# Strassen's seven products for queries, keys and merge gates in a hybrid decoder block

## The chip, the cores and the metric

The kernel runs on one core of a Trainium2 chip. The metric is the device time of one execution in microseconds (us), the median over repeated executions; lower is better.

## The reference, cut to what matters

One decoder layer over 1,024 tokens of width 1,024, in float32. The part that the change touches is the input projection `z = u @ w_in`, whose columns belong to seven consumers:

```python
u = rms_norm(x, g_mix)
z = u @ w_in
xr, gr, q, k, v, fl, m_lru, m_attn = split(z)      # 1024 columns each, fl has 8
h = rg_lru(causal_depthwise_conv(xr, ...), ...)     # gates from xc, then a linear recurrence in time
y_lru = (h * gelu(gr)) @ w_lru_out
log_f = log_sigmoid(fl + b_forget)                  # its running sum is a bias of the attention scores
o = forgetting_attention(q, k, v, log_f)            # 8 heads of 128
merged = sigmoid(m_lru) * y_lru + sigmoid(m_attn) * (o @ w_attn_out)
x = x + merged @ w_out
x = x + hierarchical_moe(rms_norm(x, g_ffn), ...)   # 32 experts, two for each token
out = rms_norm(x, g_final)
```

## The kernel before

Every float32 matrix product is made of three products of a 32-bit format that TensorE takes quickly: each operand is split into a high and a low part, and high by high, high by low and low by high are summed. ScalarE makes a high part by a copy, VectorE the low part by a subtraction. `u` is held turned, as `uh` and `ul` (128 partitions, 8 chunks of the width, 1,024 tokens).

The projection is made in blocks of 256 columns of `w_in`. `load_block` brings a block into one of two slots, `split_hi` and `split_lo` split it. `product` makes 128 of its columns against all tokens: 8 chunks x 3 products x 2 token halves = 48 matmuls of 128x512. A block is two such products, `c` = 0 and 1. `product_rows` (values) has tokens on the partitions: 24 matmuls of 128x256 for each of 8 token tiles of a block.

The stages follow each other with a barrier of all engines at the end of each (`stage`):

- `norm_in` (line 215): RMSNorm, turning and splitting of `u`, and the first product of the next stage.
- `lru_qk` (line 356): four turns. Each makes a block of XR, a block of GR, the 48 matmuls of the recurrence's gates (line 465), a block of keys and a block of queries. The convolution, the gates' functions and the recurrence's scan (lines 557 to 586) run on VectorE and ScalarE beside the products of the same turn.
- `value` (line 596): four blocks of values, 32 tiles.
- `merge_gates` (line 672): eight blocks of merge gates with a sigmoid, and the forget gate: 48 matmuls with 8 columns of `w_in` as weights, its logarithm on 8 partitions x 1,024 tokens, its running sum by a scan.
- `branch_out(0)` (line 813): splits `mix`, the recurrence's output, into `uh` and `ul`, and multiplies by `w_lru_out`. Then follow `attention`, `branch_out(1)`, `project_route` and `experts`, untouched but for two waits.

Stages are tied over their barriers in this way: the last product that TensorE makes in a stage is often the first of the next one, so that TensorE has work up to the barrier. `merge_gates` has none after its last block, and `branch_out(0)` can't start before it has split `mix`. Queries, keys, values and gates go to DRAM (`qk_d`, `v_d`, `sig_d`) and are read back in later stages. The semaphores of these stores outlive a stage.

Of the kernel before, what the change touches and what calls it, by code (L numbers as in the profile page):

```python
# [26 lines left out]
F32 = mybir.dt.float32  # L27
# [23 lines left out]
NEG = -3.0e38  # L51

# [38 lines left out]
class Kernel:  # L91
    def __init__(self, nc, ins, out):
# [47 lines left out]
        self.v_mm = [self.sem(f"v_mm{s}") for s in range(2)]  # L140
# [7 lines left out]
        self.sig_stored = [stores(f"sig{s}") for s in range(2)]  # L148
# [66 lines left out]
    def norm_in(self):  # L215
# [23 lines left out]
        with nc.Block() as block:  # L239
            @block.sync  # L240
            def _(sp):
                for t in range(NT):
                    sp.dma_start(xt[:, t, :], k_.x[t * P:(t + 1) * P, :]).then_inc(x_loaded[t], 16)
                for s, col in enumerate((XR, GR)):
                    k_.load_block(sp, s, 0, k_.w_block(k_.w_in, col))
# [110 lines left out]
    def lru_qk(self):  # L356
# [5 lines left out]
        p0, self.pairs = self.pairs, self.pairs + 2 * turns  # L362
# [16 lines left out]
        st = [work.put(f"qk_{c}", [P, 2, T], F32R) for c in range(2)]  # L379
        SCALE = (1.0, -HD ** -0.5)  # L380
# [4 lines left out]

        qk_hi, qk_lo = ([[sem(f"qk_{n}{g}{c}") for c in range(2)] for g in range(2)] for n in ("hi", "lo"))
        qk_stored = k_.qk_stored
# [7 lines left out]
        w_c = (k_.w_first, k_.w_used)  # L395

        with nc.Block() as block:
            @block.sync
            def _(sp):
                def gates(i):  # L400
                    sp.wait_ge(rg_lo, i)
# [3 lines left out]
                def store(i, g, c):  # L405
                    sp.wait_ge(qk_lo[g][c], i + 1)
                    part = 2 - 2 * g

                    head = 2 * i + c if g == 0 else i + i + c
                    sp.dma_start(k_.qk_d[head][:, part:part + 2, :], st[c][:, :, :].bitcast(F32))\  # L410
                        .then_inc(qk_stored[c], 16)

                def turn(i, last):
                    for s, col in enumerate((KC, QC)):
                        k_.load_block(sp, s, p0 + 2 * i + 1, k_.w_block(k_.w_in, col + WB * i))
                    if not last:
                        gates(i + 1)
                    for s, col in enumerate((XR, GR)):
                        store(i, s, 0)
                        k_.load_block(sp, s, p0 + 2 * i + 2, k_.w_block(k_.w_in, VC + WB * s if last else col + WB + WB * i))  # L420
                        store(i, s, 1)
                gates(0)
                with sp.Fori(0, turns - 1) as i:
                    turn(i, False)
                turn(turns - 1, True)

            @block.gpsimd
            def _(pool):
# [5 lines left out]
                for i in range(turns):  # L434
                    for ready in (*xr_out, *gr_out, *qk_hi[0]):
                        if blocks == MAXX:
                            break
                        pool.wait_ge(ready, i + 1)
# [7 lines left out]
            def _(pe):  # L446
                def products(i, s, pair, read, count, cs=(0, 1)):

                    pe.wait_ge(k_.w_lo[s], p0 + 2 * i + pair + 1)
                    for c in cs:  # L450
                        pe.wait_ge(read[c], count)
                        k_.product(pe, k_.ps[c], s, c).then_inc(w_c[c][s], 1)

                def turn(i):
                    products(i, 1, 0, xr_out, i + 1)
                    pe.wait_ge(rg_lo, i + 1)
                    pe.wait_ge(xcl_done, 2 * i + 2)
                    for m in range(2):
                        for g in range(2):
                            pe.wait_ge(gate_out[g], 2 * i + m)  # L460
                            for kk in range(2):
                                for w, u, first, last in ((rg_h, xc_h, kk == 0, False), (rg_h, xc_l, False, False),
                                                          (rg_l, xc_h, False, kk == 1)):
                                    for h in range(2):
                                        mm = pe.matmul(k_.ps[2 + g][:, h * HALF:(h + 1) * HALF],
# [3 lines left out]
                    products(i, 0, 1, gr_out, i + 1)  # L469
                    products(i, 1, 1, qk_lo[0], i + 1)  # L470

                products(0, 0, 0, qk_lo[1], 0, (1,))
                turn(0)
                with pe.Fori(1, turns) as i:
                    products(i, 0, 0, qk_lo[1], i)
                    turn(i)
                pe.wait_ge(k_.w_lo[0], self.pairs + 1)
                for g in range(2):
                    pe.wait_ge(gate_out[g], 2 * turns)
                for t in range(2):  # L480
                    k_.product_rows(pe, k_.value_ps(t), 0, t, k_.uh, k_.ul).then_inc((k_.w_first[0], k_.v_mm[0])[t], 1)

            @block.scalar
            def _(act):
                def xr_copy(i, c):
                    act.wait_ge(w_c[c][0], p0 + 2 * i + 1)
                    act.activation(xr[:, c, pad:pad + T], k_.ps[c][:, :], ACT.Copy).then_inc(xr_out[c], 1)
# [5 lines left out]
                def gelu(i, c):  # L493
                    act.wait_ge(w_c[c][1], p0 + 2 * i + 1)
                    act.activation(gl[:, c, :], k_.ps[c][:, :], ACT.Gelu_apprx_tanh).then_inc(gr_out[c], 1)

                def qk_high(i, g, c):
                    act.wait_ge(w_c[c][g], p0 + 2 * i + 2)
                    act.wait_ge(qk_stored[c], 16 * (2 * i + g))
                    act.activation(st[c][:, 0, :], k_.ps[c][:, :], ACT.Copy, scale=SCALE[g]).then_inc(qk_hi[g][c], 1)  # L500

                with act.Fori(0, turns) as i:
                    k_.split_hi(act, 1, p0 + 2 * i)
                    act.wait_ge(mixed, 2 * i)
                    xr_copy(i, 0)
                    act.wait_ge(rg_loaded, 32 * (i + 1))
                    act.wait_ge(gate_mm[1], 2 * i)
# [3 lines left out]
                    k_.split_hi(act, 0, p0 + 2 * i + 1)  # L511
# [3 lines left out]
                    for m in range(2):  # L515
                        act.wait_ge(gate_mm[0], 2 * i + m + 1)
                        act.activation(a_sb[:, m, :], k_.ps[2][:, :], ACT.Sigmoid, bias=cur[:, m, PBA:PBA + 1])\
                            .then_inc(gate_out[0], 1)
                        act.wait_ge(gate_mm[1], 2 * i + m + 1)
                        act.activation(i_sb[:, m, :], k_.ps[3][:, :], ACT.Sigmoid, bias=cur[:, m, PBX:PBX + 1])\  # L520
                            .then_inc(gate_out[1], 1)
                    for m in range(2):
                        act.wait_ge(gate_out[0], 2 * i + m + 1)
                        act.activation(rt_sb[:, m, :], a_sb[:, m, :], ACT.Tanh, scale=cur[:, m, PS:PS + 1])\
                            .then_inc(t_done, 1)
                    for m in range(2):
                        act.wait_ge(t_done, 2 * i + m + 1)
                        act.activation(a_sb[:, m, :], a_sb[:, m, :], ACT.Exp, scale=cur[:, m, PN:PN + 1])\
                            .then_inc(a_done, 1)
                    act.activation(rt_sb[:, :, :], rt_sb[:, :, :], ACT.Sqrt).then_inc(root, 1)  # L530
                    k_.split_hi(act, 1, p0 + 2 * i + 1)
                    for c in range(2):
                        qk_high(i, 0, c)
                    k_.split_hi(act, 0, p0 + 2 * i + 2)
                    for c in range(2):
                        qk_high(i, 1, c)

            @block.vector
            def _(dve):
                PER = 15  # L540

                def qk_low(i, g, c):
                    dve.wait_ge(qk_hi[g][c], i + 1)
                    dve.scalar_tensor_tensor(out=st[c][:, 1, :], in0=k_.ps[c][:, :], scalar=SCALE[g],
                                             in1=st[c][:, 0, :].bitcast(F32), op0=ALU.mult,
                                             op1=ALU.subtract).then_inc(qk_lo[g][c], 1)

                dve.wait_ge(zeroed, 1)
                with dve.Fori(0, turns) as i:
                    steps = Steps(dve, own, i * PER)  # L550
                    dve.wait_ge(a_done, 2 * i)
# [1578 lines left out]
```

## Time and profile before

| what | value |
|---|---|
| median of 3 runs | 1825.11 us (1822.89 to 1829.03) |
| profiled execution: its time, its span | 1828.22 us, 1826.5 us |
| busy share of the span | TensorE matmul 93%, VectorE 57%, ScalarE 46% |
| mean granted TensorE clock | 0.973 of full speed |
| `lru_qk`, `value`, `merge_gates` | 42.5 to 707.5 us, TensorE busy 660.6 of 665.0 us |
| experts | from 1204.7 us on, DMA busy 98% |

TensorE's matmuls are pipelined: one of 128x512 lasts 390 ns in the profile, but the next one starts before it ends. The price of one is therefore the distance of starts, read from rows of the timeline. A granted clock of 1.00 is 2.4 GHz and one of 0.5 is 1.2 GHz.

### The profile page before, as it was taken

What the parts mean: (1) busy time and instruction counts of PE and PEld (TensorE: products, weight loads), DVE (VectorE), ACT (ScalarE), POOL (GpSimd) and SP (SyncE); (2) the same over time, 40 slices, a digit from 0 to 9 for tenths busy, and PEclk for the clock granted to TensorE, in tenths of its full rate; (3) what the DMA queues carried; (4) which work ended last, traced back from release to release, by engine and by line L of the source; (5) the groups of instructions that cost most, each with busy time, mean ns of one, the idle gap of its engine ahead of it and who ended that gap; (6) DMA issues with size and microseconds to landing.
All of it is one profiled execution on the core that took longest, in us unless ns stands there. A gap on an engine that the chain in (4) does not pass through costs nothing. (4 is left out here: it accounts for less than half of the span.)

```text
span 1826.5 us, 22589 instructions
## 1 busy us (share of the span) xinstructions
PE 1703.8 (93%) x8515; PEld 1364.1 (75%) x8515; DVE 1037.0 (57%) x1125; ACT 840.3 (46%) x845; POOL 137.6 (8%) x187
## 2 busy tenths in 40 slices
PE   5999999999999998999888999969999999999991
PEld 4888888889987887878777888846667777777760
DVE  4353444432213313247665433769988888888886
ACT  5433334241122212036553111247777777878772
POOL 1000000000000000011110000110000000000005
PEclk9999999999999999999999999979999999999995
DMA  4343333323331223546655240379999999999977
GB/s 151 93 153 95 109 96 131 115 100 111 134 132 63 92 93 137 183 154 230 212 170 180 92 166 36 121 285 391 399 390 398 392 398 392 392 399 392 398 293 280
DMA packets 151686, 390.36 MB, mean 214 GB/s; under 512 B 14009, under 2 KB 73481, under 8 KB 147537
## 3 DMA queue, kind: packets, MB, share of 16 engines
q1 hardware_dynamic: 138368, 343.20, 51.0%
q0 software_dynamic: 8384, 29.63, 5.1%
q10 hardware_dynamic: 4880, 16.82, 2.3%
q8 instruction: 34, 0.56, 0.1%
q14 instruction: 20, 0.16, 0.0%
HBM read 322.15 MB, written 67.46 MB: 213 GB/s over the span
## 5 line engine op out<-in xcount | busy, mean ns | idle before, releaser
L1608 DVE TENSOR_TENSOR e_l<-e_raw,e_h 128x2048 fp32r<-128x2048 f32 x192 | 439.2, 2290 | 64.8 <-ACT e_h L1602 64.5
L1602 ACT ACTIVATE e_h<-e_raw 128x2048 fp32r<-128x2048 f32 x192 | 367.8, 1917 | 84.9 <-PE ps L1637 50.2
L199 PE MATMUL ps<-uh,w_h 128*128 128x512 f32 x1008 | 312.9, 392 | 11.9 <-DVE ul L908 9.7
L199 PE MATMUL ps<-ul,w_h 128*128 128x512 f32 x1008 | 312.1, 391 | 0.0
L199 PE MATMUL ps<-uh,w_l 128*128 128x512 f32 x1008 | 311.7, 391 | 0.0
L183 DVE TENSOR_TENSOR w_l<-w_raw,w_h 128x2048 fp32r<-128x2048 f32 x38 | 87.1, 2292 | 328.5 <-ACT w_h L179 328.5
L199 PEld LDWEIGHTS ps<-uh,w_h 128*128 128x128 f32 x1008 | 189.8, 189 | 52.8 <-issue 13.2
L199 PEld LDWEIGHTS ps<-ul,w_h 128*128 128x128 f32 x1008 | 190.2, 189 | 39.8
L199 PEld LDWEIGHTS ps<-uh,w_l 128*128 128x128 f32 x1008 | 190.2, 189 | 39.7
L1624 PE MATMUL ps<-e_h,e_xth 128*96 128x512 f32 x512 | 205.1, 401 | 6.3 <-DVE e_l L1608 3.0
L1624 PE MATMUL ps<-e_h,e_xtl 128*96 128x512 f32 x512 | 202.6, 396 | 0.0
L1624 PE MATMUL ps<-e_l,e_xth 128*96 128x512 f32 x512 | 201.9, 394 | 0.0
L179 ACT ACTIVATE w_h<-w_raw 128x2048 fp32r<-128x2048 f32 x38 | 72.7, 1914 | 167.6 <-DMA w_raw<-w_in 82.6
L1624 PEld LDWEIGHTS ps<-e_h,e_xth 128*96 128x96 f32 x512 | 83.0, 162 | 46.4 <-issue 7.3
L1624 PEld LDWEIGHTS ps<-e_h,e_xtl 128*96 128x96 f32 x512 | 83.1, 162 | 36.0
L1624 PEld LDWEIGHTS ps<-e_l,e_xth 128*96 128x96 f32 x512 | 83.4, 163 | 31.9
L1637 PE MATMUL ps<-e_h,e_hth 128*96 128x512 f32 x256 | 82.6, 404 | 2.1 <-DVE e_htl L1758 2.1
L1637 PE MATMUL ps<-e_l,e_hth 128*96 128x512 f32 x256 | 80.3, 395 | 0.0
L1637 PE MATMUL ps<-e_h,e_htl 128*96 128x512 f32 x256 | 80.2, 394 | 0.0
L1689 POOL DMA_INDIRECT e_xg<-xn_d,slots_i x30 | 41.3, 1378 | 474.2 <-PE ps L1700 474.2
L211 PE MATMUL ps<-w_h,uh 128*128 128x256 f32 x256 | 72.6, 284 | 0.9 <-PEq L164 0.9
L1097 PE MATMUL ps<-at_qk 128*128 128x512 f32 (+3 forms) x288 | 71.2, 378 | 2.3 <-PEq L164 2.0
(285 smaller groups left out, 2375.3 us busy)
## 6 DMA issues: line engine op xcount, KB each, us to landing
e_raw<-w_exp_gate SPq DMA_DIRECT2D x64, 1024.0 KB, 20.2
e_raw<-w_exp_up SPq DMA_DIRECT2D x64, 1024.0 KB, 20.1
e_raw<-w_exp_down SPq DMA_DIRECT2D x64, 1024.0 KB, 19.5
w_raw<-w_in SPq DMA_DIRECT2D x28, 1024.0 KB, 5.6
qk_d<-qk SPq DMA_DIRECT2D x16, 1024.0 KB, 4.2
at_qk<-qk_d SPq DMA_DIRECT2D x8, 2048.0 KB, 11.6
y_d<-e_y ACTq DMA_DIRECT2D x32, 384.0 KB, 6.5
y_d<-zeros POOLq DMA_DIRECT2D x22, 384.0 KB, 4.2
```

The lines of the kernel that those rows point to most:

```text
L179: act.activation(self.w_h[s][:, :, :], self.w_raw[s][:, :, :], ACT.Copy).then_inc(self.w_hi[s], 1)
L183: dve.tensor_tensor(self.w_l[s][:, :, :], self.w_raw[s][:, :, :], self.w_h[s][:, :, :].bitcast(F32), ALU.subtract).then_inc(self.w_lo[s], 1)
L199: mm = pe.matmul(ps[:, h * HALF:(h + 1) * HALF], w[:, k, :], u[:, k, h * HALF:(h + 1) * HALF], start=first, stop=last)
L211: mm = pe.matmul(ps, u[:, k, rows], w[s][:, k, :], start=first, stop=last)
L1097: mm = pe.matmul(k_.ps[n % 2][:, at:end], q, qk[c][:, part, at:end], start=first, stop=last)
L1602: act.activation(self.e_h[m % SPLIT][:, :, :], self.e_raw[slot][:, :, :], ACT.Copy).then_inc(self.e_hi[m % SPLIT], 1)
L1608: dve.tensor_tensor(self.e_l[slot][:, :, :], self.e_raw[slot][:, :, :], self.e_h[m % SPLIT][:, :, :].bitcast(F32), ALU.subtract).then_inc( ...
L1624: mm = pe.matmul(ps, x[:, k, :], w[:, k, :], start=first and first_piece, stop=last and last_piece)
L1637: mm = pe.matmul(ps[:, c * HALF:(c + 1) * HALF], x[:, at, :], w[:, 2 * k + c, :], start=first, stop=last)
L1689: pool.indirect_dma_start(out=xg[b][:, :], out_offset=None, in_=k_.xn_d, in_offset=bass.IndirectOffsetOnAxis(ap=slots, axis=0)).then_inc(g ...
```

## The change

Four stages take the place of `lru_qk`, `value` and `merge_gates`; three barriers stay three.

- `first_heads`: keys and queries of the first head pair by `product` as before, the forget gate's 48 matmuls between them, its logarithm and sum now with tokens on 128 partitions (64 elements each) and the sum by two small matmuls; and VectorE makes the four sums T1 to T4 of the quarters of `u` (width halves x token halves) and splits them.
- `halves`: the other three head pairs of keys and queries and all merge gates, 14 blocks, each as Strassen-Winograd's seven half products of 12 matmuls (4 chunks x 3) instead of two products of 48. For each block VectorE makes 4 sums of the quarters of the block, 7 low parts, 7 additions of products into the four quadrants of the result, and for keys and queries 4 low parts of the result; ScalarE 7 high parts, a copy and 4 finishing copies or sigmoids. All are 128x512. Operands go round a ring of 11 tiles, products round 6 PSUM banks, the raw block has one place.
- `lru_value`: four turns of XR, GR, the recurrence's gates and one block of values. The recurrence's scan runs beside the values. Loops are written out instead of `Fori`.
- `branch_out(0)` waits for the new stores' semaphores.

```diff
+HALVED = [(kind, i) for i in range(1, D // WB) for kind in "KQ"] + [(kind, i) for i in range(D // WB) for kind in "LA"]
+RING = 11
+USED = ("A11", "S1", "S2", "A12", "S3", "S4", "A22")
+MADE = ("A11", "S1", "S2", "A12", "A22", "S3", "S4")
+BANKS = 6
+    def load_quarters(self, eng, n):
+        for c in range(2):
+            eng.dma_start(self.raw_q[:, 2 * c:2 * c + 2, :, :].rearrange("p q k n -> p (q k) n"),
+                          self.w_in.rearrange("(k p) n -> p k n", p=P)[:, :, col + c * P:col + (c + 1) * P])\
+                .then_inc(self.raw_in, 16)
+    def first_heads(self):      # SyncE
+                store(0, 0)
+                sp.wait_ge(k_.w_used[0], p0 + 1)
+                k_.load_quarters(sp, 0)
+                store(0, 1)
+                for c in range(2):
+                    store(1, c)
+                sp.wait_ge(bias_out, 1)
+                sp.dma_start(k_.bias_d.rearrange("h (t p) -> (h t) p", p=P), bias[:, :]).then_inc(k_.bias_stored, 16)
+                for c in range(2):
+                    sp.wait_ge(qk_stored[c], 16 * 2)
...
+                # VectorE, the end of first_heads
+                turned_low(T4, 4)
+                low(1, 0)
+                dve.wait_ge(f_turned, 1)
...
+                dve.wait_ge(sum_mm, 1)
+                dve.tensor_tensor(flat(c_sum), sum_ps, flat(fr), ALU.add).then_inc(sum_out, 1)
+                low(1, 1)
+    def halves(self):           # SyncE
+                def load(n):
+                    sp.wait_ge(a_lo, 7 * n - 7 + MADE.index("A22") + 1)
+                    if n < NBLOCKS:
+                        k_.load_quarters(sp, n)
+                    else:
+                        k_.load_block(sp, 0, p0, k_.w_block(k_.w_in, XR))
+                load(1)
+                for n in range(NBLOCKS):
+                    store(n, C11)
+                    if n + 2 <= NBLOCKS:
+                        load(n + 2)
+                    for q in (C22, C12, C21):
+                        store(n, q)
...
+                # TensorE
+                def part_product(n, name):
+                    pe.wait_ge(a_lo, 7 * n + MADE.index(name) + 1)
+                    bank_free(n, name)
+                    for k in range(KD // 2):
+                        for w, u, first, last in ((r_h, u_h, k == 0, False), (r_h, u_l, False, False),
+                                                  (r_l, u_h, False, k == KD // 2 - 1)):
+                            op = pe.matmul(bank(n, name), w(n, name)[:, k, :], u[:, k, :], start=first, stop=last)
+                    op.then_inc(mm, 1)
...
+                # ScalarE
+                for n in range(NBLOCKS):
+                    copy(n)
+                    high(n + 1, "A11")
+                    for name in ("S1", "S2", "A12"):
+                        high(n + 1, name)
+                    finish(n, C11)
+                    high(n + 1, "A22")
+                    finish(n, C22)
+                    high(n + 1, "S3")
+                    finish(n, C12)
+                    high(n + 1, "S4")
+                    finish(n, C21)
...
+                # VectorE
+                for n in range(NBLOCKS):
+                    for name in SUMS:
+                        add_up(n + 1, name)
+                    low(n + 1, "A11")
+                    join(n, 1, C12, C11, "S2")
+                    low(n + 1, "S1")
+                    join(n, 2, C11, C11, "A12")
+                    low(n + 1, "S2")
+                    low(n + 1, "A12")
+                    final_low(n, C11)
+                    join(n, 3, C21, C12, "S3")
+                    join(n, 4, C12, C12, "S1")
+                    join(n, 5, C22, C21, "S1")
+                    low(n + 1, "A22")
+                    low(n + 1, "S3")
+                    final_low(n, C22)
+                    join(n, 6, C12, C12, "S4")
+                    low(n + 1, "S4")
+                    final_low(n, C12)
+                    join(n, 7, C21, C21, "A22")
+                    final_low(n, C21)
+    def lru_value(self):        # TensorE
+                for i in range(turns):
+                    products(i, OF_XR, gr_out, i, (0, 1) if i > 0 else (1,))
+                    products(i, OF_GR, xr_out, i + 1)
+                    gates(i)
+                    values(i)
...
                     for m in range(2):
                         steps.did(dve.scalar_tensor_tensor(out=rt, in0=a, scalar=1.0, in1=rt, op0=ALU.add, op1=ALU.mult))
                         steps.did(dve.tensor_tensor(i_sb[:, m, :], i_sb[:, m, :], rt, ALU.mult))
+                        value_low(i, 3 + 2 * m)
+                        if m == 0:
+                            k_.split_lo(dve, *slot(i, NEXT))
                         steps.did(dve.tensor_tensor_scan(rt, a, i_sb[:, m, :], 0.0, ALU.mult, ALU.add))
+                        value_low(i, 4 + 2 * m)
+                        dve.tensor_tensor(k_.mix[:, 2 * i + m, :], rt, gl[:, m, :], ALU.mult).then_inc(mixed, 1)
+                    value_low(i, NT - 1)
...
+                for c in range(2):      # SyncE, the end of lru_value
+                    sp.wait_ge(k_.v_stored[c], 16 * NH // 2)
```

## Rows read from the trace of the kernel before

**Rows 1.** The page, busy time of TensorE's matmuls: us, share, count.
```profile
PE 1703.8 (93%) x8515; PEld 1364.1 (75%) x8515; DVE 1037.0 (57%) x1125; ACT 840.3 (46%) x845; POOL 137.6 (8%) x187
```

**Rows 2.** Busy time by stretch: lru_qk, value, merge_gates; clock, DMA share, GB/s last.
```profile
42.50:425.00 382.50, 382.47 (x1680) 315.72 (x1681) 162.42 (x119) 141.45 (x115) 17.75 (x23) 1.00 0.33 111
425.00:530.60 105.60, 103.53 (x818) 101.09 (x817) 23.16 (x37) 20.05 (x37) 0.00 (x0) 1.00 0.40 140
530.60:707.50 176.90, 174.55 (x768) 139.36 (x768) 38.48 (x22) 41.30 (x33) 0.95 (x1) 1.00 0.27 85
```

**Rows 3.** Timeline of TensorE (start, us): matmuls in norm_in and in the recurrence's gates.
```profile
35.95 0.39 PE L310 MATMUL ps<-uh,w_h 128*128 128x512 f32 x1
...
40.71 0.39 PE L310 MATMUL ps<-uh,w_h 128*128 128x512 f32 x1
...
75.29 0.63 PE L465 MATMUL ps<-lru_xch,rg_h 128*128 128x512 f32 x2
...
86.06 0.64 PE L465 MATMUL ps<-lru_xch,rg_l 128*128 128x512 f32 x2
```

**Rows 4.** Timeline of ScalarE: high parts of two neighbouring value tiles.
```profile
515.65 0.38 ACT L651 ACTIVATE v<-ps 128x256 fp32r<-128x256 f32 x1 [2.50 <-PE ps L211]
518.53 0.38 ACT L651 ACTIVATE v<-ps 128x256 fp32r<-128x256 f32 x1 [2.50 <-PE ps L211]
```

**Rows 5.** Timeline of ScalarE in the first turn of lru_qk.
```profile
86.73 1.12 ACT L520 ACTIVATE lru_xr<-ps,lru_prm 128x1024 f32<-128x1024 f32 x1 [1.70 <-PE ps L465]
87.75 2.18 ACT L524 ACTIVATE lru_rt<-lru_a,lru_prm 128x1024 f32<-128x1024 f32 x2
89.94 1.28 ACT L528 ACT_TABLE_LOAD   x1
91.24 2.19 ACT L528 ACTIVATE lru_a<-lru_a,lru_prm 128x1024 f32<-128x1024 f32 x2
...
94.74 1.92 ACT L530 ACTIVATE lru_rt<-lru_rt 128x2048 f32<-128x2048 f32 x1
```

**Rows 6.** Timeline at the barrier before branch_out(0).
```profile
704.55 0.61 PE L199 MATMUL ps<-uh,w_l 128*128 128x512 f32 x2
705.21 1.02 ACT L763 ACTIVATE m<-ps 128x1024 f32<-128x1024 f32 x1 [9.85 <-PE ps L199]
707.55 7.69 ACT L890 ACTIVATE uh<-mix 128x1024 fp32r<-128x1024 f32 x8 [1.32 <-PEq L164]
710.01 1.19 PE L199 MATMUL ps<-uh,w_h 128*128 128x512 f32 x2 [4.84 <-DVE ul L908]
...
713.45 0.62 PE L199 MATMUL ps<-ul,w_h 128*128 128x512 f32 x2
```

**Rows 7.** Groups of instructions by line and shape: busy us, mean ns, idle before.
```profile
L1161 DVE TENSOR_TENSOR at_ptl<-ps,at_pth 128x512 fp32r<-128x512 f32 x48 | 32.3, 688 | 1.4 <-ACT at_pth L1140 1.2
L328 DVE SCALAR_TENSOR_TENSOR ul<-ps,gm,uh 128x512 fp32r<-128x512 f32 x16 | 11.0, 745 | 0.2
L1140 ACT ACTIVATE at_pth<-ps 128x512 fp32r<-128x512 f32 x48 | 27.8, 596 | 12.5 <-PE ps L1106 12.5
L782 DVE TENSOR_TENSOR f_l<-f_raw,f_h 128x64 fp32r<-128x64 f32 x1 | 0.2, 218 | 0.0
L584 DVE TENSOR_TENSOR lru_xr<-lru_xr,lru_rt 128x1024 f32<-128x1024 f32 x8 | 9.8, 1225 | 0.3
L585 DVE TENSOR_TENSOR_SCAN lru_rt<-lru_a,lru_xr 128x1024 f32<-128x1024 f32 x8 | 18.3, 2292 | 0.3
```

**Rows 8.** DMA issues of a stretch: count, KB each, median us from issue to landing.
```profile
qk_d<-qk SPq DMA_DIRECT2D x16, 1024.0 KB, 4.2
v_d<-v SPq DMA_DIRECT2D x8, 1024.0 KB, 9.2
at_v<-v_d SPq DMA_DIRECT2D x2, 512.0 KB, 6.3
at_v<-v_d SPq DMA_DIRECT2D x2, 512.0 KB, 15.4
```

More of the change, by code:

```diff
@@ L354, in _, with halves_map @@
                 dve.tensor_scalar(k_.prm[:, :, PN], eq[:, :], -LRU_C, None, ALU.mult).then_inc(own, 1)
-    def lru_qk(self):
+    def halves_map(self):
+        turned = Map(self.nc, self.work_start - 4 * KD * T, self.high)
+        self.t_h, self.t_l = ([turned.put(f"wn_t{n}{part}", [P, KD // 2, HALF], F32R) for n in range(1, 5)] for part in "hl")
+        self.halves_at = turned.at
+        same = Map(self.nc, self.work_start - 4 * KD * T, self.high)
+        self.t_spare, self.t_full = ([same.put(f"wn_t{n}{part}", [P, KD // 2, HALF]) for n in range(1, 5)] for part in ("spare", "full"))
@@ L378, in lru_qk @@
         gl = work.put("lru_gl", [P, 2, T])
-        st = [work.put(f"qk_{c}", [P, 2, T], F32R) for c in range(2)]
-        SCALE = (1.0, -HD ** -0.5)
+        vst = [work.put(f"v_{part}", [P, NT, WB], F32R) for part in range(2)]
         sem = self.sem
@@ L413, in turn, with load @@
-                def turn(i, last):
-                    for s, col in enumerate((KC, QC)):
-                        k_.load_block(sp, s, p0 + 2 * i + 1, k_.w_block(k_.w_in, col + WB * i))
+                def load(i, kind, src):
+                    s, p = slot(i, kind)
+                    k_.load_block(sp, s, p, src)
+                gates(0)
+                for q in range(4):
+                    sp.wait_ge(k_.quad_stored[q], 16 * k_.quads_until(NBLOCKS))
+                load(0, OF_GR, k_.w_block(k_.w_in, GR))
@@ L416, in turn @@
+                for i in range(turns):
+                    load(i, OF_V, k_.w_block(k_.w_in, VC + WB * i))
+                    last = i == turns - 1
+                    load(i, NEXT, k_.w_block(k_.ins["w_lru_out"][0], 0) if last else k_.w_block(k_.w_in, XR + WB * (i + 1)))
                     if not last:
                         gates(i + 1)
[L418 to L425, printed above, removed]
+                    load(i + 1, OF_GR, k_.w_block(k_.ins["w_lru_out"][0], WB) if last else k_.w_block(k_.w_in, GR + WB * (i + 1)))
+                    for t in range(4):
+                        sp.wait_ge(v_lo[t], 2 * i + 2)
+                    for part in range(2):
+                        sp.dma_start(k_.v_d[i, part], vst[part][:, :, :].bitcast(F32)).then_inc(k_.v_stored[i % 2], 16)
@@ L446, in _, with products, gates @@
             def _(pe):
-                def products(i, s, pair, read, count, cs=(0, 1)):
-                    pe.wait_ge(k_.w_lo[s], p0 + 2 * i + pair + 1)
+                def products(i, kind, read, count, cs=(0, 1)):
+                    s, p = slot(i, kind)
+                    pe.wait_ge(k_.w_lo[s], p + 1)
                     for c in cs:
[L451 to L455, printed above, removed]
+                        if count > 0:
+                            pe.wait_ge(read[c], count)
+                        k_.product(pe, in_ps[c], s, c).then_inc(w_c[c][s], 1)
+                def gates(i):
                     pe.wait_ge(rg_lo, i + 1)
@@ L2105, in write @@
     def write(self):
-        for write, *args in ((self.norm_in,), (self.lru_qk,), (self.value,), (self.merge_gates,),
+        for write, *args in ((self.norm_in,), (self.first_heads,), (self.halves,), (self.lru_value,),
                              (self.branch_out, 0), (self.attention,), (self.branch_out, 1), (self.project_route,),
```

646 lines of the change are left out of this document (372 added, 274 removed).

## The prediction, made before the change was run

> **What bounds the kernel now.** I read the page first: TensorE's matmuls fill 93% of the span [rows 1]. A share over the whole span says little, so the second view is busy time by stretch. In the three stages that change, TensorE is idle for 0.03 us of 382.5, 2.07 of 105.6 and 2.35 of 176.9, all at full clock, while VectorE and ScalarE are busy for 20 to 40% of it [rows 2]. These 665 us are therefore a queue of matmuls: one that is left out is worth its full distance of starts, and every new pause of TensorE costs its full length. The third view gives that distance. The reader is to see that starts, not durations, count: 21 matmuls lie between 35.95 and 40.71 us, 0.2267 us each, and this is the form that the change uses, one 512-column matmul for each weight [rows 3]. The recurrence's gates are slower, 46 between 75.29 and 86.06, 0.2341 us [rows 3]. A value tile takes 2.88 us [rows 4].
>
> **What is taken away.** A block takes 84 matmuls instead of 96. 14 blocks save 168 x 0.2267 = **38.1 us**. XR, GR, values, the first head pair, the forget gate (48 matmuls) and the recurrence's gates keep their counts. A block of `halves` lasts 84 x 0.2267 = 19.04 us, a half product 2.72 us, and 14 blocks 266.6 us.
>
> **Does `halves` keep TensorE fed?** VectorE has 22 operations of 128x512 in a key or query block and 18 in a gate block. The nearest row is 0.69 us [rows 7] (L1161); with a wait on its own predecessor some 0.03 more. 22 x 0.69 = 15.2 us. Three times it must stand still for ScalarE, whose 128x512 takes 0.60 us [rows 7] (L1140): the low part of S3 comes after `finish(C22)` and its own high part (two operations, 1.2, one of VectorE's beside them, so 0.5), that of S4 after `finish(C12)` (1.2), the last `final_low` after `finish(C21)` (0.6). That makes 17.6 us against 19.04. The chain that could stop TensorE is a bank: A11 of the next block needs the bank of S1, read last by join 5. S3's product ends at 13.6 us of the block, three joins later it is 15.8, and the bank is wanted at 19.04: 3.2 us to spare. Operands are ready more than 9 us ahead. At the 0.745 of L328 [rows 7] the cycle is 16.4 + 2.3 + waits = 19.0, still level. I take nothing, and keep up to +7 us for the range.
>
> The raw block has one place. Its load is issued after the low part of A22 and wanted by the sum S1: 15 VectorE operations (10.4 us) and the landing must fit into 19.04, so the landing may take 8.5 us. The nearest row is the pair of loads with 512-byte pieces, 2 x 512 KB: 6.3 us, and 15.4 in the worst case beside other transfers [rows 8]. I take 6.3 (the quiet queue is the likelier likeness: stores of 1.5 MB follow it, they do not precede it), so nothing; the upper end is a rival below. ScalarE has 12 x 0.60 = 7.2 us in a block.
>
> The start costs something. The first load is issued only when the first block's A22 is split; VectorE waits for it and reaches join 5 about 0.5 us late; S1's low part is 0.5 late; and after a pause the clock is at its lower level: from 710.01 to 713.45 eight matmuls took 3.44 us instead of 1.81 [rows 6], 1.6 more. **+2.6 us.**
>
> **The end of `first_heads`.** Count from its start. TensorE: K's second product, forget gate, Q's first, 3 x 10.88 = 32.7; eight small transposes 0.7; Q's second: 44.3 us. VectorE starts at 3.2 (one copy, one split on ScalarE); eight sums and five splits of 2,048 elements (twice a 1,024-element L584 less its start, 2.3 [rows 7]) are 30.3; two low parts and the bias addition 3.8; the next low part 1.2: 38.5. Then the forget gate's chain: some 12 operations of 64 elements at 0.22 [rows 7] (L782), a reciprocal, seven smaller ones, and on ScalarE two table loads of 1.28 [rows 5] with a short activation each: 7 us, 45.5. Two small matmuls, one addition, the last low part: 47.2. The store that follows takes 4.2 [rows 8], and SyncE waits for it before the barrier; the barrier itself 1.3 (from 706.23 to 707.55 [rows 6]); the first high and low part of `halves` 1.4: 54.1. TensorE stands for 9.8 us, less 0.1 for its small matmuls, and 0.7 earlier: 10.4. The old barrier there cost 0.9 of the 2.07 us: **+9.5 us**. In short, a chain on VectorE and a store that were hidden behind eight more blocks are now the last thing before a barrier. Bounds: 7 (the sums overlap the start better) and 13.
>
> Of table loads, the Trainium skill (ScalarE: Activation LUTs, What ACT_TABLE_LOAD costs) says that each switch drains the engine for about 1.38 us beside the load. The trace shows no such time: the tanh ends at 89.93, the load starts at 89.94 and the exponential at 91.24 [rows 5]. By the page the sum would be 2.8 us higher; by the row it is as above.
>
> **`halves` to `lru_value`.** XR's first product is made before the barrier and hides the last stores. Behind it GR's load waits for those stores and for two small loads in SyncE's queue; with 6.3 landing, a split of 1.9 and 2.3, GR is ready at about the time when TensorE ends XR (10.9 us). Barrier 1.1 and 0.5 of waiting against 1.2 for the old one: **+0.4 us**. Bounds 0 and +4.
>
> **A turn of `lru_value`.** Gates 11.25 us, eight tiles 23.0. Tile 7 needs the low part of tile 3. Count from the gates' start, 75.29 in the old turn: the last sigmoid starts at 11.4, as before [rows 5]. ScalarE now waits for tile 2 (20.1) ahead of the root, which ends at 23.7 instead of 21.4. VectorE then has two recurrence steps, the low part of tile 3 (26.6) and so on; TensorE wants tile 7's bank at 31.4. No wait, nothing.
>
> **The end of `lru_value`.** From 23.7 VectorE has, for two halves, 2 x 1.23, a scan 2.3, a product 1.2 [rows 7] (L584, L585), five low parts of 0.42 and one block split 2.3: 40.2. TensorE's last tile ended at 34.3. Then SyncE stores 2 x 1 MB and waits. One such store alone takes 4.2, two behind another megabyte 9.2 [rows 8]; halfway, 6.7, and 0.5 for the second issue: 47.5. Barrier 1.3; first split of `mix`, 2.46 until TensorE starts (707.55 to 710.01 [rows 6]): 51.3. TensorE stands 17.0 us where it stood 5.0 (704.94 to 710.01): **+12.0 us**. Bounds +8 and +15. The recurrence's tail and the values' store had four and two further stages to hide in; now `branch_out(0)`, which needs `mix` and starts with an empty TensorE, follows directly.
>
> **Sum.** -38.1 + 2.6 + 9.5 + 0.4 + 12.0 = -13.6 us. The sum is made against the profiled 1828.22 us (span 1826.5), 3.1 above the median. Difference applied to the median: 1825.1 - 13.6 = **1811.5 us**. Everything after `branch_out(0)` starts is the same work at the same distances.
>
> **Rivals.**
> 1. VectorE becomes the bound in `halves`. For it: 17.6 of 19.04 us, and a start without reserve. Against it: the row of 0.69 has PSUM as input like the joins. If an operation costs 0.80 with its waits, a cycle is 20.1 plus handovers, 20.6; 6 key and query blocks lose 1.6 each less 2.8 of reserve: +6.8, **1818**. It decides from 0.76 on. Chance 0.15.
> 2. The raw block's round trip is the bound, and the kernel ends slower. For it: one place for the block, 512-byte pieces, four times as many store instructions behind it, and the 15.4 row. Every us of landing above 8.5 costs 14 us over the blocks. At 10.2, between the rows of 6.3 and 15.4, +23.8: **1835**. It is slower than before from 9.5 on. Chance 0.12.
> 3. Matmuls in `halves` start at the distance of the recurrence's gates. 1,176 x 0.0074 = +8.7: **1820**, no measurable change. Against it: L310 has the same shapes and change of weights. Chance 0.10.
> 4. The clock falls inside `halves`. If short pauses between the 98 groups put TensorE at the lower level half of the time, 588 matmuls take twice 0.2267, +133: **1945**. Against it: idle pauses of 1 us at the barriers left the granted clock at 1.00 [rows 2]. The Trainium skill has this rule (TensorE: Matmul & The Clock Gate, A second HAM failure mode: psum-queue depth-cycling): going round PSUM banks makes pauses that let the clock oscillate. Chance 0.02.
> 5. The two new pauses are shorter than I count (the lower bounds): -8 more, **1804**. Chance 0.09.
>
> The forecast itself has 0.52.
>
> **How the numbers follow.** A measurement of this kernel tells about 0.3%, 5.5 us, from no change. Faster (below 1819.6): 0.52 + 0.09, rival 1's 0.12 and a third of rival 3: 0.76, cut to 0.73 for stalls that I may not have seen. Same: the rest of rivals 1 and 3, 0.12. Slower: rivals 2 and 4, 0.15 with unseen ones. The range reaches down to rival 5 and up over rivals 1 and 3 into the beginning of rival 2: 1803 to 1827. The likeliest case alone: 1806 to 1818.
>
> **What would show it.** In the profile after: TensorE busy without idle through 14 blocks of about 19.0 us, each of 84 matmuls; VectorE's idle in `halves` put down to TensorE (joins 1 to 3) and not to the raw block's DMA; a pause of TensorE near 10 us some 44 us after `first_heads` starts, released by VectorE and a store; another near 17 us before `branch_out(0)`. Wrong would be: A11's matmuls waiting for VectorE's joins (rival 1), VectorE's first sum waiting for the raw load (rival 2), starts 0.234 apart (rival 3), a granted clock below 1 in `halves` (rival 4).

## The result and the profile after

The changed kernel takes 1811.62 us (median of 5 runs, 1807.05 to 1814.6) beside 1827.37 us of the kernel before (5 runs, 1822.89 to 1829.95) on the same chip: a ratio of 0.9912, 95% interval 0.9888 to 0.9936. A later series (beside experiment 6) gave 0.9888, interval 0.9870 to 0.9906. Forecast were 1811.5 us, -13.6 us and a chance of 0.73 for faster. The medians differ by 15.75 us and not by 13.6, because the kernel before came out 2.3 us above the 1825.1 that the forecast started from: that 1811.62 lies 0.1 us from the forecast is luck. The profiled execution has a span of 1811.0 us where the one before had 1826.5.

The page of the changed kernel, busy time, answers to [rows 1]:

```profile
PE 1672.3 (92%) x8360; PEld 1336.6 (74%) x8360; DVE 1181.9 (65%) x1395; ACT 881.2 (49%) x969; POOL 136.5 (8%) x187
```

VectorE has 145 us more work and TensorE 31.5 us less. Busy time by stretch of the changed kernel (TensorE, its weight loads, VectorE, ScalarE, GpSimd, then granted clock, DMA share, GB/s). In order: `first_heads`, its end, a block of keys or queries, a block of gates, the start of `lru_value`, the barrier before `branch_out(0)`. It answers to [rows 2].

```profile
42.50:88.00 45.50, 44.67 (x202) 31.57 (x201) 38.20 (x37) 15.67 (x13) 0.11 (x1) 1.00 0.27 94
88.00:97.50 9.50, 1.46 (x9) 1.05 (x8) 2.38 (x4) 1.91 (x3) 0.00 (x0) 0.65 0.29 114
173.40:192.50 19.10, 19.10 (x86) 15.83 (x85) 14.29 (x22) 6.94 (x13) 0.00 (x0) 1.00 0.51 166
268.60:287.70 19.10, 19.10 (x86) 15.82 (x85) 11.80 (x18) 7.17 (x13) 0.00 (x0) 1.00 0.36 111
384.00:396.00 12.00, 10.06 (x37) 7.81 (x36) 7.61 (x6) 4.46 (x4) 0.96 (x1) 0.86 0.39 129
690.00:712.00 22.00, 14.77 (x55) 12.05 (x56) 12.60 (x10) 9.50 (x9) 0.00 (x0) 0.73 0.40 156
```

The reader is to see that inside a block of `halves` TensorE is busy for all of 19.10 us at full clock, with VectorE busy for 14.3, and that the idle time lies in three places: behind `first_heads`, at the start of `lru_value`, and before `branch_out(0)`. From the first matmul behind the barrier ahead of these stages to the first of `branch_out(0)` the kernel before took 667.48 us (42.53 to 710.01), the changed one 653.42 (43.81 to 697.23): **-14.06 us**. What lies ahead came 1.3 us later, what follows took 1113.8 us instead of 1116.5; in the twelve profiles of changed and experimental kernels of this study that rest, which is the same work, takes 1110.1 to 1116.7, so it is no effect of the change. This stretch, called the changed stretch below, is what the experiments are read by: it is steadier than the time of a run.

Every stop of TensorE of over 0.4 us in it, timeline of the changed kernel (start, us, tile; in brackets the idle time before and what ended it):

```profile
97.31 0.80 PE L656 MATMUL ps<-uh,wn_ah 128*128 128x512 f32 x1 [7.72 <-DVE wn_al L730]
...
377.53 0.70 PE L208 MATMUL ps<-uh,w_h 128*128 128x512 f32 x2 [0.70 <-PEq L173]
...
390.63 0.73 PE L208 MATMUL ps<-uh,w_h 128*128 128x512 f32 x2 [1.94 <-DVE w_l L192]
...
697.23 1.19 PE L208 MATMUL ps<-uh,w_h 128*128 128x512 f32 x2 [15.22 <-DVE ul L1132]
```

These are 25.58 us of stops. The kernel before had 0.87, 1.22 and 4.84 us at its three barriers, 6.93: +18.65 us. The rest, -14.06 - 18.65 = -32.7 us, is in the stream of matmuls: -38.1 for 168 matmuls fewer, and 5.4 given back, mostly by the lower clock behind the stops.

The end of `first_heads`, timeline of the changed kernel, shows which chain is last:

```profile
85.60 1.45 DVE L561 TENSOR_TENSOR d_before<-d_before,d_fr 128x8 f32<-128x8 f32 x7
...
88.42 0.33 PE L466 MATMUL ps<-d_fr,stri 128*128 128x64 f32 x2
...
88.62 1.02 ACT L477 ACTIVATE qk<-ps 128x1024 fp32r<-128x1024 f32 x1 [5.30 <-PE ps L208]
...
89.68 1.22 DVE L506 SCALAR_TENSOR_TENSOR qk<-ps,qk 128x1024 fp32r<-128x1024 f32 x1 [0.44 <-ACT qk L477]
90.93 0.32 SPq L429 DMA_DIRECT2D qk_d<-qk  x1
91.29 0.54 SPq L437 DMA_DIRECT2D bias_d<-d_bias  x1
...
95.91 0.63 ACT L675 ACTIVATE wn_ah<-wn_raw 128x512 fp32r<-128x512 f32 x1 [6.01 <-PEq L173]
```

The forget gate's sums are done at 87.05, before TensorE ends the last query product at 88.4. What ends last is that product itself, its high and low part, and its store (90.93 to the barrier ahead of 95.91).

The end of `lru_value`, the same view:

```profile
683.08 2.28 DVE L1032 TENSOR_TENSOR_SCAN lru_rt<-lru_a,lru_xr 128x1024 f32<-128x1024 f32 x1
...
685.73 1.22 DVE L1034 TENSOR_TENSOR mix<-lru_rt,lru_gl 128x1024 f32<-128x1024 f32 x1
686.87 0.42 DVE L987 TENSOR_TENSOR v<-ps,v 128x256 fp32r<-128x256 f32 x1
687.37 0.81 SPq L848 DMA_DIRECT2D v_d<-v  x2
694.77 7.69 ACT L1114 ACTIVATE uh<-mix 128x1024 fp32r<-128x1024 f32 x8 [12.34 <-PEq L173]
```

TensorE's last value matmul starts at 681.73. Then come VectorE's tail (to 687.29), the store of 2 x 1 MB with its wait and the barrier (to 694.77), and the first splits of `mix`, 2.46 us: the three parts of the forecast, in its order. Waits inside `halves` (engine, line, whom it waited for: us in total, times, longest):

```profile
DVE wn_stl L740 <- PE ps L656: 34.3, 30, 6.2
DVE wn_al L730 <- ACT wn_ah L675: 29.5, 27, 5.7
DVE wn_as L724 <- DMA wn_raw<-w_in: 16.4, 7, 4.6
...
PE ps L656 <- DVE wn_al L730: 7.7, 1, 7.7
```

TensorE's one wait is its start; VectorE has time to wait for TensorE, for ScalarE and for the load. Seven times its first sum waits for the raw block; this reaches no matmul.

### The profile page after: what moved, and what is told of

Its sections match the earlier page's. It is cut to its first block and busy times, and to the rows that moved or that the text cites. A ratio compares the mean times of both kernels' runs of the same rounds, so it can differ in the third digit from the quotient of the medians.

```text
span 1811.0 us, 22778 instructions
## 1 busy us (share of the span) xinstructions
PE 1672.3 (92%) x8360; PEld 1336.6 (74%) x8360; DVE 1181.9 (65%) x1395; ACT 881.2 (49%) x969; POOL 136.5 (8%) x187
## 5 line engine op out<-in xcount | busy, mean ns | idle before, releaser
L208 PE MATMUL ps<-uh,w_h 128*128 128x512 f32 x560 | 175.5, 395 | 24.7 <-DVE ul L1132 21.2
L208 PE MATMUL ps<-ul,w_h 128*128 128x512 f32 x560 | 175.0, 394 | 0.0
L208 PE MATMUL ps<-uh,w_l 128*128 128x512 f32 x560 | 173.9, 392 | 0.0
L208 PEld LDWEIGHTS ps<-uh,w_h 128*128 128x128 f32 x560 | 105.6, 190 | 48.1 <-issue 23.2
L208 PEld LDWEIGHTS ps<-ul,w_h 128*128 128x128 f32 x560 | 106.6, 190 | 22.6
L208 PEld LDWEIGHTS ps<-uh,w_l 128*128 128x128 f32 x560 | 106.6, 190 | 22.5
L188 ACT ACTIVATE w_h<-w_raw 128x2048 fp32r<-128x2048 f32 x24 | 45.9, 1912 | 113.8 <-DMA w_raw<-w_in 46.4
L192 DVE TENSOR_TENSOR w_l<-w_raw,w_h 128x2048 fp32r<-128x2048 f32 x24 | 54.9, 2289 | 58.6 <-ACT w_h L188 58.6
L740 DVE TENSOR_TENSOR wn_stl<-wn_stl,ps 128x512 f32<-128x512 f32 x98 | 67.0, 684 | 39.2 <-PE ps L656 34.3
```

The lines of the kernel that those rows point to most:

```text
L188: act.activation(self.w_h[s][:, :, :], self.w_raw[s][:, :, :], ACT.Copy).then_inc(self.w_hi[s], 1)
L192: dve.tensor_tensor(self.w_l[s][:, :, :], self.w_raw[s][:, :, :], self.w_h[s][:, :, :].bitcast(F32), ALU.subtract).then_inc(self.w_lo[s], 1)
L208: mm = pe.matmul(ps[:, h * HALF:(h + 1) * HALF], w[:, k, :], u[:, k, h * HALF:(h + 1) * HALF], start=first, stop=last)
L740: dve.tensor_tensor(out, part, bank(n, name), ALU.add).then_inc(added, 1)
```

## The experiments

Each kernel is the changed one with one edit. Times are medians; ratios are against the kernel before on the same chip.

**1. The saved matmuls, put back.**

```diff
+                    for again in range(2 if name == "S2" else 1):
                         for k in range(KD // 2):
```

> Of every block of halves, TensorE makes the product S2 twice (the second overwrites the first), so that a block has 96 matmuls as in the kernel before; the output is the same. Theory (the number of matmuls sets the time of halves): 14 x 12 x 0.2267 = +38.1 us over the changed kernel, 1850, a block 21.8 us. Rival (part of the saving is lost to VectorE or the raw block, which would now get 2.7 us more for each block): less than +30.

Measured: 1844.68 us, ratio 1.0105 (1.0086 to 1.0123). From the first matmul of `halves` to the first behind its barrier it is 96.31 to 414.64, 318.33 us, where the changed kernel has 97.31 to 377.53, 280.22: +38.11 us. The whole changed stretch is only 35.6 us longer (689.03 against 653.42), because the stop at GR was 1.05 us here and brought no lower clock. A block lasts 21.8 us, full:

```profile
170.00:191.80 21.80, 21.80 (x98) 18.03 (x97) 14.33 (x23) 7.04 (x13) 0.00 (x0) 1.00 0.44 145
```

So the whole of the saving arrives in `halves`. It also gives the size of the rest: with 96 matmuls a block the new order costs 1.05% more than the old.

**2. VectorE's room.** Two kernels repeat the low parts of the three direct operands, once (3 operations more in a block) and twice (6 more).

```diff
+                    for again in range(1 if name in direct else 0):    # 2 in the second kernel
+                        repeats.did(dve.tensor_tensor(r_l(n, name), source(n, name), r_h(n, name).bitcast(F32), ALU.subtract))
                     dve.tensor_tensor(r_l(n, name), source(n, name), r_h(n, name).bitcast(F32), ALU.subtract).then_inc(a_lo, 1)
```

> VectorE makes the low parts of A11, A12 and A22 twice in every block of halves: 3 more operations of 128x512, with a wait each about 2.1 us a block; the output is the same. Theory (VectorE has 1.7 us of slack in a block of keys or queries, and a reserve of 2.8 us built up beside it): 6 such blocks lose 0.4 each, covered by the reserve: 0 to +1 us. Rival (VectorE is the bound already): +12. Rival (VectorE's waits give way, there is far more room): 0 here and also with six operations.

> The same low parts three times in every block of halves: 6 more operations, about 4.2 us a block; the output is the same. Theory: a block of keys or queries takes 2.5 us more than TensorE's 19.04, six of them 15, less 2.8 of reserve: +12 us, and the 8 gate blocks, with four operations fewer, cost nothing. Rival (VectorE is the bound already): +58 over all 14 blocks, or +25 over six. Rival (far more room): 0.

Measured: 1814.73 us, ratio 0.9945 (0.9928 to 0.9962), and 1831.05 us, 1.0031 (1.0018 to 1.0044). The changed stretch is 655.10 us (+1.7) and 674.09 (+20.7), where 0 to +1 and +12 were expected. With three, TensorE stops once in `halves` after its start, 2.58 us at 121.09, between the first block and the second; that stop, the lower clock behind it (1.6) and 0.7 more at the start are set off by a stop at GR of only 0.40 us, without the lower clock. With six it stops at the start of nearly every block, and what releases it is always a join (timeline; two blocks of keys and queries, two of gates):

```profile
187.30 0.47 PE L656 MATMUL ps<-uh,wn_ah 128*128 128x512 f32 x1 [1.39 <-DVE wn_stl L743]
...
207.99 0.47 PE L656 MATMUL ps<-uh,wn_ah 128*128 128x512 f32 x1 [1.36 <-DVE wn_stl L743]
...
349.51 0.47 PE L656 MATMUL ps<-uh,wn_ah 128*128 128x512 f32 x1 [0.56 <-DVE wn_stl L743]
...
369.30 0.47 PE L656 MATMUL ps<-uh,wn_ah 128*128 128x512 f32 x1 [0.50 <-DVE wn_stl L743]
```

In blocks of keys and queries rival 1 is a real mechanism with the place that the prediction gave it, A11 behind the joins. Such a block takes 207.99 - 187.30 = 20.69 us, for 22 + 6 operations and the waits for ScalarE, and VectorE waits neither for TensorE nor for the load. The repeats of A11 and A12 add 0.72 each (the 0.69 and the wait on itself); the two of A22 add 0.74 together, because they run where VectorE otherwise waits 0.62 for ScalarE. That is 3.6, so the changed kernel's own cycle is 20.69 - 3.6 = 17.1 us, against 19.04 of TensorE.

Gate blocks, counted at nothing, lost 0.75 each (19.79 against 19.04), and there the joins are only the last link. VectorE stands idle for 2.2 us before its first sum and waits for the raw block (timeline of the second kernel):

```profile
351.44 1.02 SPq L382 DMA_DIRECT2D wn_raw<-w_in  x2
...
357.34 0.69 DVE L725 TENSOR_TENSOR wn_as<-wn_raw 128x512 f32<-128x512 f32 x1 [2.21 <-DMA wn_raw<-w_in]
```

The repeats lengthen the way from that sum to the low part of A22 to 13.9 us (357.34 to 371.20), only then is the next load issued, and it takes 5.9: 19.8 a block. So these eight blocks show rival 2, and the kernel doesn't separate the two rivals as cleanly as the expectation had it.

**3. The raw block, later.**

```diff
-                    store(n, C11)
-                    if n + 2 <= NBLOCKS:
-                        load(n + 2)
-                    for q in (C22, C12, C21):
+                    for q in (C11, C22, C12, C21):
                         store(n, q)
+                        if q == C12 and n + 2 <= NBLOCKS:
+                            load(n + 2)
```

> The load of the raw block is issued after the store of C12 in place of after that of C11, five VectorE operations and ScalarE's waits later (5.4 us for keys and queries, 2.5 for gates); the output is the same. Theory (the raw block's round trip): 10.4 from the sum S1 to the low part of A22, 5.4, and a landing of 4.9 make 20.7 to 21.4 us against 19.04: 6 blocks lose 1.7 to 2.4 each, less a reserve of 3: +7 to +11 us; gate blocks (17 us) nothing. Rival (the load has more room than I count, as VectorE's order bends round it): 0 to +2. Rival (a later load collides with the stores and lands late): +25 and more.

Measured: 1831.67 us, ratio 1.0045 (1.0030 to 1.0060); the changed stretch 673.39 us, +20.0, twice what I expected. Timeline of this kernel:

```profile
146.99 1.18 SPq L382 DMA_DIRECT2D wn_raw<-w_in  x2
...
153.94 0.69 DVE L723 TENSOR_TENSOR wn_as<-wn_raw 128x512 f32<-128x512 f32 x1 [5.83 <-DMA wn_raw<-w_in]
...
163.60 0.47 PE L655 MATMUL ps<-uh,wn_ah 128*128 128x512 f32 x1 [2.02 <-DVE wn_stl L739]
```

The store of C12 is two DMA instructions, 0.9 us of SyncE's queue, and from the issue of the first of the two loads to the sum that needs both it is 6.95 us, not the 4.9 of the median landing of one. 10.1 (sum to low part) + 5.0 + 0.9 + 6.95 = 22.95 us a block; measured are 22.4 to 23.0. Six stops make 15.9 us, and behind four of them the clock was at the lower level (the stretch from the stop on, columns as above; beside it a stop without):

```profile
140.64:145.60 4.96, 4.96 (x15) 3.96 (x16) 3.13 (x6) 2.19 (x4) 0.00 (x0) 0.66 0.28 106
163.60:168.60 5.00, 5.00 (x22) 4.16 (x23) 3.16 (x6) 2.19 (x4) 0.00 (x0) 1.00 0.19 66
```

15 matmuls instead of 22 in 5 us cost 1.6 us. That makes 15.9 + 4 x 1.6 + some 0.26 for each of the six restarts, less the 3.6 of the stop at GR, which doesn't occur here: 20.3. So rival 2 is real too. In the changed kernel the load has 8.9 us of room (19.04 - 10.1), and its pair takes 5.7 to 7.2 us from the first issue to the last landing: at worst 1.7 us to spare, a little less than VectorE's 1.9.

**4. The forget gate as before, on 8 partitions.** The transposes, the small matmuls and the 64-element form are replaced by:

```diff
+                dve.tensor_tensor_scan(c_sum[:, :], ones[:, :], f[:, :], 0.0, ALU.mult, ALU.add).then_inc(sum_out, 1)
+                sp.wait_ge(k_.bias_stored, 16)
```

> The forget gate's logarithm and running sum stay in first_heads, but as the kernel before made them: 8 partitions x 1,024 tokens and a scan, without the transposes and the two small matmuls, and SyncE waits for the bias's store before the barrier; the output is the same. Theory (VectorE's chain after the sums is what ends last before the barrier): some 12 operations of 1,024 elements at 1.2 to 2.3 us, about 20 us in place of 6, of which some 1.4 were hidden: TensorE's pause at the end of first_heads grows from 7.7 to about 20, +12 us. Rival (the store of the last query quarter and the barrier set the pause, VectorE's chain is hidden): 0 to +3.

Measured: 1819.44 us, ratio 0.9967 (0.9956 to 0.9979); `halves` starts 65.66 us after `first_heads`, not 53.50: +12.2. The stop is 21.71 us. Its largest part (timeline):

```profile
87.47 6.54 DVE L544 RECIPROCAL d_dw<-d_dw 8x1024 f32<-8x1024 f32 x1
...
94.05 1.21 DVE L545 TENSOR_TENSOR d_eq<-d_eq,d_w 8x1024 f32<-8x1024 f32 x1
```

The edit also makes SyncE wait for the bias's store. From the issue of the query store to ScalarE's start behind the barrier it is 5.27 us here (102.52 to 107.79) and 4.98 in the changed kernel, so that wait accounts for at most 0.3 of the 12.2. The token partitions are worth 12 us in this place: without them the whole change would be nearly nothing (0.33% faster). In the changed kernel this reciprocal takes 0.55 us.

**5. Three waits and orders around the stops, one at a time.** (a) SyncE doesn't wait for the values' stores at the end of `lru_value`. (b) GR's load ahead of `gates(0)`. (c) `split_hi` and `split_lo` of the next block before the root and the scan.

```diff
-                for c in range(2):                                             # (a)
-                    sp.wait_ge(k_.v_stored[c], 16 * NH // 2)
...
+                load(0, OF_GR, k_.w_block(k_.w_in, GR))                        # (b)
                 gates(0)
-                load(0, OF_GR, k_.w_block(k_.w_in, GR))
...
                         steps.did(dve.tensor_tensor(i_sb[:, m, :], i_sb[:, m, :], xc[:, m, :], ALU.mult))
+                        if m == 0:                                             # (c)
+                            k_.split_lo(dve, *slot(i, NEXT))
```

> At the end of lru_value SyncE doesn't wait for the stores of the values (the next stage but one reads them and waits itself, as before); the output is the same. Theory (the store of 2 x 1 MB, 687.4 to about 694, is what ends last before the barrier): the pause of 15.2 us before branch_out(0) shrinks by 5 to 6 us, and the time with it. Rival (VectorE's tail and the barrier set it): 0 to -1. Rival (branch_out(0)'s loads queue behind the stores and give it back): -2 to 0.

> At the start of lru_value the first GR block is loaded ahead of the two small loads for the recurrence's gates; the output is the same. Theory (GR is 1.94 us late, because its load waits in SyncE's queue, and the lower clock after that pause costs another 1.7): -2 to -3.6 us. Rival (GR waits for the stores of halves, not for the queue): 0.

> In lru_value, ScalarE and VectorE split the next block (high part and low part, 128x2048) before the recurrence's root and scan in place of between them; in the last turn the block is branch_out's first; the output is the same. Theory (VectorE's tail, 682 to 687 us, stands between TensorE's last matmul and the values' store): the tail is 2.3 us shorter, -2.3 us. Rival (VectorE's tail then waits for the last value tiles instead, which end only at 681.7): -1 to 0.

(a) 1801.74 us, ratio 0.9869 (0.9854 to 0.9883); the stop before `branch_out(0)` is 9.60 us, -5.6, and nothing is given back. The changed stretch is 648.34 us, -5.1, because the stop at GR was 2.67 us this time. The store has the same place; `uh` starts 1.8 us after it and not 7.4:

```profile
686.20 0.81 SPq L848 DMA_DIRECT2D v_d<-v  x2
687.98 7.69 ACT L1112 ACTIVATE uh<-mix 128x1024 fp32r<-128x1024 f32 x8 [6.72 <-PEq L173]
```

(b) 1806.38 us, 0.9895 (0.9881 to 0.9910), in time no different from the changed kernel; there is no stop at GR, and the changed stretch is 649.55 us, -3.9, or -1.5 against the changed kernel's second profile (below). (c) 1808.99 us, 0.9917 (0.9904 to 0.9930), in time no different from the changed kernel; the stop is 13.39 us, -1.8. Its stretch is 649.24, but 2.4 of the -4.2 come from a shorter stop at GR (1.15 us), which has nothing to do with the edit: the changed kernel run again shows the same, below.

**6. The last query store behind the barrier, all four together, and the changed kernel again.**

```diff
-        st = [work.put(f"qk_{c}", [P, 2, T], F32R) for c in range(2)]
+        st = [Map(nc, self.halves_at + at, self.high).put(f"qk_{c}", [P, 2, T], F32R)
+              for c, at in enumerate((0, 4 * (2 * RING - 4) * KD // 2 * P))]
...
-                for c in range(2):
-                    sp.wait_ge(qk_stored[c], 16 * 2)
+                sp.wait_ge(qk_stored[0], 16 * 2)
...
+                        if n == 1:      # VectorE in halves, before the sum S1
+                            dve.wait_ge(self.qk_stored[1], 16 * 2)
```

> The last query product of first_heads is stored from a buffer that lies over ring places which halves writes only in its second block, so that SyncE doesn't wait for this store before the barrier and VectorE waits for it a block later; the output is the same. Theory (the store, 90.9 to about 94.6, ends last before the barrier behind first_heads): the pause of 7.7 us shrinks to about 4.2, -3.5 us. Rival (the bias's chain and the barrier set it): -0.5 to 0.

> Four edits together: no wait for the values' stores at the end of lru_value, GR's load ahead of the two small loads, the block split before the recurrence's root and scan, and the last query store behind the barrier; the output is the same. Theory (each takes its own part of a pause in which nothing else runs): from the start of first_heads to the first matmul of branch_out(0) 653.4 - 5.6 - 1.8 - 3.8 - 3.5 = 638.7 us, about 1797 us. Rival (the pauses give way to each other or to a new wait): -8 us or less against the changed kernel, 1803 and more.

> The changed kernel once more, on the chip of the two runs beside it: 1811 us; from the start of first_heads to the first matmul of branch_out(0) 653.4, less up to 1.9 where the pause before GR doesn't bring the lower clock.

The store alone: 1808.43 us, ratio 0.9900 (0.9881 to 0.9919); stop 4.81 instead of 7.72 us, -2.9 where -3.5 was expected; in time not to be told from the changed kernel. The changed kernel again: 1806.59 us, 0.9888; stretch 651.02, with a stop of 1.14 us at GR and no lower clock behind it, 2.4 less than in its first profile. All four: **1794.65 us, ratio 0.9835 (0.9817 to 0.9854)**, faster than both kernels; its stretch is 43.73 to 682.29, 638.56 us, where 638.7 was expected. Its stops:

```profile
94.36 0.79 PE L657 MATMUL ps<-uh,wn_ah 128*128 128x512 f32 x1 [4.82 <-DVE wn_al L733]
...
374.26 0.70 PE L208 MATMUL ps<-uh,w_h 128*128 128x512 f32 x2 [0.70 <-PEq L173]
...
682.29 1.19 PE L208 MATMUL ps<-uh,w_h 128*128 128x512 f32 x2 [7.40 <-DVE ul L1134]
```

The stops lie in different places with nothing else running, so their savings add. That the sum is met to 0.1 us is partly chance: against the changed kernel's second profile the same four edits are worth 12.5 us, not 14.9.

## Why the prediction was right, step by step

| step | forecast, us | measured, us |
|---|---|---|
| 168 matmuls fewer | -38.1 | -38.1 (experiment 1) |
| start of `halves` | +2.6 | +1.9 (14 blocks in 268.5 against 266.6) |
| end of `first_heads` | +9.5 | +8.7 (8.89 of stop, 0.68 of transposes, less 0.87) |
| `halves` to `lru_value` | +0.4 | +3.1 (stops of 0.70 and 1.94, 1.7 of lower clock, less 1.22) |
| end of `lru_value` | +12.0 | +10.4 (15.22 less 4.84) |
| sum | -13.6 | -14.0 (the changed stretch: -14.06) |

The mechanism was right, and the sum better than its parts: three terms were put 0.7, 0.8 and 1.6 us too high and one 2.7 too low, which nearly cancels.

- **The bound.** That TensorE's queue sets these stages [rows 2] held: one product more in each block cost its matmuls in full, to 0.1 us. The distance of 0.2267 from [rows 3] held for weights that change with every matmul: 19.04 us a block. Rival 3 didn't come.
- **Start of `halves`.** The 1.9 us are the restart at the lower clock alone (12 matmuls in 4.62 us instead of 2.72). VectorE's late start, put at 2 x 0.5, reached no matmul.
- **VectorE.** The conclusion held, the size was 0.5 us too large: 17.6 us forecast, 17.1 by experiment 2. Join 5 ends 2.8 us before the next block's A11 wants its bank (191.59 and 194.43), where 3.2 were forecast. An operation of 128x512 lasts 0.69, but where it needs nothing of the one before it, the next one starts 0.60 later (158.05, 158.65, 159.25 in experiment 3's kernel). Durations were summed where starts should have been, the mistake that the text avoids for TensorE. The three waits for ScalarE are there, as 0.62, 1.22 and 0.70 us in each such block.
- **The raw block.** The forecast took 6.3 us and allowed 8.5; measured are 5.7 to 7.2 and 8.9. At worst this leaves 1.7 us of room, not the 2.2 that it gave. Rival 2 was priced soundly, and experiment 3 shows it, with a surcharge for the clock. But its sign was badly chosen: VectorE's first sum did wait for the raw load, seven times and 16.4 us in all, in a kernel in which the load costs nothing. VectorE is ahead of TensorE and waits for whatever comes last; only a wait of A11's matmuls would have told.
- **End of `first_heads`.** The sum was nearly right (53.5 us against 54.1) by a chain that wasn't quite the one named. VectorE is done with the forget gate 2.2 us sooner than counted, so it is hidden behind the last query product, and that product's own split and store come last. Experiment 4 shows how little it takes for the named chain to be last.
- **`halves` to `lru_value`.** The worst-sized term. The arrival of GR was put at 0.5 us late; it was 1.94 late in one profile and 1.14 in another of the same kernel, and the first of them brought the lower clock: 12 matmuls in 4.44 us instead of 2.72. Landing (7.7 us from issue to ScalarE's start, behind the two small loads) was counted as 6.3; in the ten profiles with this order of loads it took 5.4 to 8.4, with GR ahead of them 5.2 and 5.3. The bound of +4 covered it; experiment 5b takes the term away.
- **End of `lru_value`.** 17.0 us forecast, 15.2 measured: tail, store and barrier in the order given, the store shorter than the 6.7 taken between the two rows of [rows 8] (median landing 4.9). Experiment 5a shows that the store, not VectorE, is the last link.
- **The clock.** TensorE goes round six PSUM banks in 98 groups and the granted clock is 1.00 from 103 to 377 us, the whole of `halves` behind its start, so rival 4 is wrong. The Trainium skill's rule (TensorE: Matmul & The Clock Gate, A second HAM failure mode: psum-queue depth-cycling) describes pauses between groups; here there are none as long as VectorE is in time.

For the late GR the trace of before had no row: it has no load for whose arrival TensorE waits at the start of a stage.

## What to carry to other kernels

A cut in the number of matmuls pays in full where TensorE never waits, but the reordering that allows it puts tails (a scan, a split, a store waited for at a barrier) next to stages that can't start without them; here they took back 24 of 38 us, of which waits and orders alone gave back 14.9 (653.42 to 638.56, 3.6 of them at GR, which came out 2.4 cheaper in the changed kernel's second profile). Ask of every store waited for at a barrier who reads it or writes over it next: a wait there rather than at the barrier gave 5.6 and 2.9 us. Count distances of starts on VectorE as on TensorE, and a pair of loads from the first issue to the last landing.

## What the runs showed of the hardware

- A stop of about 2 us can bring TensorE to the lower level. Behind stops of 1.94, 2.17, 2.58 and 2.67 us the granted clock of the next 5 us was 0.66 to 0.68; behind 1.74, 1.84, 1.90 and 2.02 it was 1.00. As 1.94 fell and 2.02 didn't, length alone doesn't decide; what else does is not shown. In experiment 3, after a stop of 3.45 us, matmuls started 0.23 us apart for 1.0 us and only then slowed down. Each such fall cost some 1.6 us: 12 matmuls took 4.34 to 4.44 us behind these four stops and 2.81 to 2.88 behind the four others. Of the 2.4 us between the two profiles of the changed kernel it is the larger part.
- VectorE's reciprocal is far dearer for each element than the other functions here: 6.54 us for 1,024 elements of a partition, where an operation on two tensors takes 1.21 and the scan 2.28.
- Table loads followed the activation before them at once, as in [rows 5]: in the changed kernel an exponential of 0.26 us starts at 81.49, the load of 1.28 us at 81.76. The drain of about 1.38 us for each switch, by the Trainium skill (ScalarE: Activation LUTs, What ACT_TABLE_LOAD costs), and with it the term of 2.8 us, didn't appear.
